# Modulations in pairs, a norm in two token parts and head reciprocals per token in a hybrid diffusion step

## What is computed

```python
def trunk_layer(x, cond, p, lam_init, ctx):
    shift1, scale1, gate1, shift2, scale2, gate2 = modulation(cond, p['w_mod'], p['b_mod'])   # 6 x 1024 per condition
    h = rmsnorm(x, p['g_mix']) * (1 + scale1) + shift1
    rq, rk, rv, rg, wq, wk, wv, dq, dk, dv, mcq, mckv, mkr = split(h @ p['w_in'])              # 2720 columns
    o_ret  = head_layernorm(bidirectional retention) * silu(rg)                               # head norm 1
    o_win  = window attention with a sink
    o_diff = rmsnorm(differential attention, p['g_diff']) * (1 - lam_init)                    # head norm 2
    o_mla  = multi-head latent attention
    merged = sum of sigmoid(h @ w_gate[n] + b_gate[n]) * (o_n @ w_branch[n])
    x = x + gate1 * (merged @ p['w_out'])
    h = rmsnorm(x, p['g_ffn']) * (1 + scale2) + shift2
    u = conv3(h @ p['w_up'] + b_up)                                                            # 2 x 2816 columns
    x = x + gate2 * ((u1 * silu(u2)) @ p['w_down'])
```

## Time and profile before

| | |
|---|---|
| median of 3 runs | 2518.57 us (2517.09 to 2520.24) |
| the profiled execution | 2514.07 us |
| its span, first to last instruction | 2512.2 us |
| mean granted TensorE clock | 0.975 |
| PE busy | 2397.0 us (95%) |
| DVE, ACT, POOL busy | 1239.9, 899.2, 754.9 us |

### The profile page before, as it was taken

The page is one execution under the profiler, slowest core; times in us unless marked ns, Lnnn a source line. Parts: engine busy times, 40 slices in busy tenths (PEclk is TensorE's granted clock), DMA queues, the critical chain, the costliest instruction groups (busy, mean ns, idle before and its releaser), DMA issues.

```text
span 2512.2 us, 38193 instructions
## 1 busy us (share of the span) xinstructions
PE 2397.0 (95%) x16007; PEld 2154.8 (86%) x16007; DVE 1239.9 (49%) x2136; ACT 899.2 (36%) x1652; POOL 754.9 (30%) x516
## 2 busy tenths in 40 slices
PE   5998999999998999999989899998999989999998
PEld 4887787778898999999968768886889989999998
DVE  4336437544235771753733461575433467536456
ACT  3424335544224431332243342555332153323221
POOL 1321131101232453544323202210113335444432
PEclk7999999999998999999989999999999989999999
DMA  8312222132321322221272132222233212222221
GB/s 284 134 37 70 95 86 89 45 101 77 105 80 52 100 68 84 68 85 59 76 243 70 36 118 63 72 74 88 68 101 94 83 51 68 84 68 85 68 68 51
DMA packets 234152, 216.45 MB, mean 86 GB/s; under 512 B 8310, under 2 KB 217598, under 8 KB 233726
## 3 DMA queue, kind: packets, MB, share of 16 engines
q1 hardware_dynamic: 225911, 193.76, 24.3%
q10 hardware_dynamic: 8071, 20.25, 2.5%
HBM read 204.92 MB, written 9.08 MB: 85 GB/s over the span
## 4 chain that ended last, share of the span: by engine, by line
PE 88%; DVE 5%; ACT 3%; issue 2%; DMA 1%; POOL 1%; ACTq 0%; DVEq 0%; SPq 0%
PE ps L744 58%; PE ps L800 12%; PE ps L839 4%; PE ps L892 2%; PE ps L871 2%; PE ps L909 2%; PE ps L755 2%; PE ps L881 2%; PE ps L1137 1%; POOL w_lo L701 1%; DVE stat L1753 1%; DVE o_rms L1959 1%; PE ps L765 1%; DMA raw<-in_w_mod 1%; PE ps L860 1%
## 5 line engine op out<-in xcount | busy, mean ns | idle before, releaser
L701 POOL TENSOR_TENSOR w_lo<-raw,w_hi 128x512 fp32r<-128x512 f32 (+1 forms) x512 | 754.7, 1504 | 1723.1 <-ACT w_hi L1283 1080.8
L744 PE MATMUL ps<-h_hi,w_hi 128*128 128x320 f32 x2432 | 631.5, 315 | 10.5 <-DVE h_lo L1700 8.0
L744 PE MATMUL ps<-h_lo,w_hi 128*128 128x320 f32 x2432 | 619.0, 310 | 0.0
L744 PE MATMUL ps<-h_hi,w_lo 128*128 128x320 f32 x2432 | 618.6, 310 | 0.0
L744 PEld LDWEIGHTS ps<-h_hi,w_hi 128*128 128x128 f32 x2432 | 425.9, 189 | 16.9 <-POOL w_lo L701 8.5
L744 PEld LDWEIGHTS ps<-h_lo,w_hi 128*128 128x128 f32 x2432 | 425.2, 189 | 0.8
L744 PEld LDWEIGHTS ps<-h_hi,w_lo 128*128 128x128 f32 x2432 | 424.7, 189 | 0.0
L1283 ACT ACTIVATE w_hi<-raw 128x2048 fp32r<-128x2048 f32 (+2 forms) x112 | 207.5, 1853 | 322.9 <-PE ps L744 241.4
L800 PE MATMUL ps<-w_hi,h_hi 128*128 128x512 f32 (+1 forms) x480 | 180.9, 377 | 17.4 <-DVE h_lo L1700 15.1
L1753 DVE TENSOR_REDUCE stat<-ps 128x1 f32<-128x640 f32 (+3 forms) x160 | 107.8, 674 | 168.7 <-PE ps L881 104.4
L1991 DVE SCALAR_TENSOR_TENSOR x<-ps,mod,x 128x128 f32<-128x128 f32 (+4 forms) x192 | 72.2, 433 | 218.8 <-PE ps L744 218.5
(11 more groups left out here) (262 smaller groups left out, 3279.3 us busy)
## 6 DMA issues: line engine op xcount, KB each, us to landing
raw<-in_w_mod SPq DMA_DIRECT2D x48, 1024.0 KB, 5.3
raw<-in_w_up SPq DMA_DIRECT2D x88, 512.0 KB, 4.8
raw<-in_w_gate SPq DMA_DIRECT2D x32, 1024.0 KB, 5.4
raw<-in_w_in SPq DMA_DIRECT2D x20, 1024.0 KB, 5.0
raw<-in_w_down SPq DMA_DIRECT2D x16, 1024.0 KB, 4.7
w_br<-in_w_branch ACTq DMA_DIRECT2D x8, 1024.0 KB, 4.9
raw<-in_w_out SPq DMA_DIRECT2D x8, 1024.0 KB, 5.1
raw<-in_w_down SPq DMA_DIRECT2D x8, 768.0 KB, 4.1
```

What stands on the lines that cost most here:

```text
L701: ins = nc.gpsimd.tensor_tensor(w_lo[s % WS][:, c0:c1], raw[u % RAW][:, c0:c1], w_hi[s % WS][:, c0:c1].bitcast(F32), ALU.subtract)
L744: ins = mm(out, w_at(w_hl[wi]), at_(x_hl[xi]), start=first and q == 0, stop=final and q == 2)
```

## The change

- The first eight modulations are made in four pairs (p, p+4), the shift and the scale of the same 256 channels. Both products go into one PSUM region (the condition columns of the second are shifted by two), one row copy, one fold with four columns, two additions and the scale of two k-steps follow. Pair 0 stands before the norm's spread and pair 1 behind it; pairs 2 and 3 and the folds of 1 to 3 stand inside `in_product(0)`. The unit order is mod 0, 4, in (0,0), mod 1, 5, 2, 6, in (0,1), mod 3, 7, and so on. The small loads move from before `in (0,1)` to before `in (1,0)`.
- At the start of layer 0 DVE copies x from PSUM, and ACT squares the unturned x with a running sum per token (five instructions of 1024 columns), so that PE's token sums aren't needed there.
- Output tiles 4 to 7 are made in two token parts, 256 and 384 tokens, all of part 0 first. The second norm is made for each part, and the first two up tiles too, part 0 of both, then part 1 of both. The first of them runs all high-high products first, then low-high, then high-low, with the sums and the spread of part 1 in between.
- Both head norms sum squares to one number per token and head (128 tokens x 20), take root and reciprocal of that, DVE copies each reciprocal 64 times along the free dimension, and PE turns the result, 128 x 128 tiles, into the layout of the outputs. In the second, the `rope` now stands before the two products.

```diff
-    units = mods(8) + win(0) + win(1) + gate(0, 0) + gate(0, 1) + win(2)
+    first, second = win(0)
+    units = mods(2) + [first] + mods(4) + [second] + mods(2) + win(1) + gate(0, 0) + gate(0, 1) + win(2)
...
+OUT_TILES = [(m, None) for m in range(4)] + [(m, 0) for m in range(4, KD)] + [(m, 1) for m in range(4, KD)]
+CUT = 2 * P
...
-                    if li == 0 and (kind, i) == ("in", (0, 1)):
+                    if li == 0 and (kind, i) == ("in", (1, 0)):
                         load_small(0)
...
+                def mod_pair(p):
+                    c0 = pair_col(p)
+                    if p >= 2:
+                        pe.wait_ge(mod_done.sem, now(mod_done, p))
+                    for second, i in enumerate((p, p + 4)):
+                        w = raw_unit("mod", i)
+                        for k in range(KD):
+                            q0 = 32 * (k % 4)
+                            last = mm(ps[q0:q0 + 32, c0:c0 + 256], cond_c[:, k, 2 - 2 * second:34 - 2 * second], w[:, k, :],
+                                      start=second == 0 and k < 4, stop=second == 1 and k >= 4)
+                        last.then_inc(mod_mm.sem, 1)
...
+                def head_sums(sq_, b):
+                    for c2 in range(2):
+                        for t in range(T):
+                            c0 = 2 * (T * c2 + t)
+                            last = mm(bank(b, c0, c0 + 2), sq_[:, c2, t * P:(t + 1) * P], c("side"), start=True, stop=True)
+                    return last
+                def turn_rstd(rec, c2, b):
+                    for t in range(T):
+                        last = tr(bank(b, t * P, t * P + P), rec[:, T * c2 + t].rearrange("p j d -> p (j d)"), ident)
+                    return last
...
-                mod_unit(0)
-                mod_unit(1)
-                pe.wait_ge(vec_done.sem, now(vec_done, 1))
-                mod_transpose(0)
+                mod_pair(0)
                 if li:
                     pe.wait_ge(x_down.sem, counts(li - 1)(x_down, 24))
-                for i in range(2, 8):
-                    mod_unit(i)
-                    mod_transpose(i - 1)
-                    if i == (2 if li else 4):
-                        token_sums(0)
-                    if i == (4 if li else 6):
-                        spread_rstd(0)
-                mod_transpose(7)
+                    token_sums()
+                fold_pair(0)
+                spread_rstd()
+                mod_pair(1)
                 pe.wait_ge(vec_done.sem, now(vec_done, 1))
-                in_product(0)
+                in_product(0, behind=[lambda: fold_pair(1), lambda: mod_pair(2), lambda: fold_pair(2), lambda: mod_pair(3), lambda: fold_pair(3)])
...
-                for c2 in range(2):
-                    ve.wait_ge(rv_act.sem, now(rv_act, c2 + 1))
-                    V.reciprocal(ret_sq[:, c2, :], ret_sq[:, c2, :]).then_inc(vstep.sem, 1)
+                def widen(rec):
+                    V.reciprocal(st5[:, 3, :], st5[:, 2, :]).then_inc(vstep.sem, 1)
+                    ve.wait_ge(vstep.sem, step())
+                    return V.tensor_copy(rec[:].rearrange("p a j d -> p (a j) d"), st5[:, 3, :].unsqueeze(2).to_broadcast([P, 4 * T, 64]))
...
-                rstd(1)
-                norm(1)
+                for m, part in OUT_TILES[:9]:
+                    take_out(m, part)
+                rstd(1, 0, 2)
+                take_out(5, 1)
+                part_norm(0, range(3))
+                take_out(6, 1)
+                part_norm(0, range(3, KD + 1))
+                take_out(7, 1)
+                rstd(2, 2, T)
+                part_norm(1, range(KD + 1))
```

More of the change, by code:

```diff
@@ L121, in shape_constants @@
     return out
+MOD_ORDER = [i for p in range(4) for i in (p, p + 4)] + list(range(8, 24))
 def weight_units():
-    mod = iter(range(24))
+    mod = iter(MOD_ORDER)
     win = lambda g: [("in", (g, half), True) for half in range(2)]
@@ L780, in spread_rstd, with part_sums, spread_part, in_product @@
                     last.then_inc(bc_mm.sem, 1)
-                def in_product(g, between=None):
+                def part_sums(part):
+                    pe.wait_ge(ss_done[1].sem, now(ss_done[1], part + 1))
+                    for t in PART_TILES[part]:
+                        last = mm(bank(4 + part, t, t + 1), ss[:, t * P:(t + 1) * P], ones[:, 0:1], start=True, stop=True)
+                    last.then_inc(ss_mm.sem, 1)
+                def spread_part(part):
+                    pe.wait_ge(diag_done.sem, now(diag_done, part + 2))
+                    for q, t in enumerate(PART_TILES[part]):
+                        last = mm(bank(6 + part, q * P, q * P + P), ones[:], diag[:, t, :], start=True, stop=True)
+                    last.then_inc(bc_mm.sem, 1)
+                def in_product(g, between=None, behind=()):
                     n, base = G_COLS[g][1], Z_BASE[g]
@@ L1094, in _ @@
                     last.then_inc(mla_mm.sem, 1)
+                pe.wait_ge(ox_done.sem, now(ox_done, 1))
+                for c2 in range(2):
+                    turn_rstd(o_rec, c2, slot()).then_inc(mla_mm.sem, 1)
                 w = raw_unit("ukv")
@@ new lines, in norm_step @@
+                def norm_step(k, done, cols, pieces):
+                    sc.wait_ge(t1_done.sem, now(t1_done, done + k + 1))
+                    if k >= 2:
+                        sc.wait_ge(h_done.sem, now(h_done, done + k - 1))
+                    i = 1 if done else 0
+                    for w, c0, c1 in pieces:
+                        ins = act_(hf[:, k % 2, c0:c1], t1[:, k % 2, c0:c1], ACT.Identity, bias=mod[:, 24 * i + k, w:w + 1],
+                                   scale=scl[:, i, k, w:w + 1])
+                    ins.then_inc(hf_done.sem, 1)
+                    sc.wait_ge(hf_done.sem, now(hf_done, done + k + 1))
+                    act_(h_hi[:, k, cols], hf[:, k % 2, cols], ACT.Copy).then_inc(hh_done.sem, 1)
@@ L1315, in norm, with part_norm @@
+                def part_norm(part):
+                    ts_ = PART_TILES[part]
+                    sc.wait_ge(ss_mm.sem, 3 * li + part + 1)
+                    act_(st5[:, 0, ts_.start:ts_.stop], bank(4 + part, ts_.start, ts_.stop), ACT.Sqrt, bias=eps_c[:], scale=1.0 / D).then_inc(rms_done.sem, 1)
+                    if part == 0:
                         round_unit()
-                        round_unit()
-                    else:
-                        round_unit()
-                    sc.wait_ge(scl_done.sem, now(scl_done, i + 1))
+                        sc.wait_ge(scl_done.sem, now(scl_done, 5))
@@ L1327, in norm @@
[L1327 to L1329 removed]
+                        norm_step(k, 8 + 8 * part, PARTS[part], ((1, CUT, TOK),) if part else ((0, 0, CTX), (1, CTX, CUT)))
                 def take_z(g, tiles=range(T)):
@@ new lines, in scale, with rstd @@
+                def scale(i, k0, n):
+                    g0 = (GMIX, GFFN)[i] + k0
+                    stt(scl[:, i, k0:k0 + n], mod[:, 24 * i + 8 + k0:24 * i + 8 + k0 + n, :], 1.0,
+                        vcol[:, g0:g0 + n].unsqueeze(2).to_broadcast([P, n, 2]), ALU.add, ALU.mult).then_inc(scl_done.sem, 1)
+                def rstd(done, t0, t1_):
+                    n = t1_ - t0
+                    ve.wait_ge(rms_done.sem, now(rms_done, done + 1))
+                    V.reciprocal(st5[:, 1, t0:t1_], st5[:, 0, t0:t1_]).then_inc(vstep.sem, 1)
```

413 lines of the change are left out of this document (237 added, 176 removed).

## The result

The changed kernel takes 2505.2 us, the median of five runs, where the kernel before takes 2518.9 beside it: a ratio of 0.9944, with a 95% interval of 0.9933 to 0.9955. A second series gave 2499.8 beside 2518.7, 0.9929 (0.9909 to 0.9949). So it is faster, by 14 to 19 us. Forecast were 41.4, and 2505.2 lies above the stated range of 2463 to 2494, and 2499.8 does too.

The account below looks back on a forecast made before the run. PE was taken to bound the kernel, except in stretches bound by chains of small steps over engines. Gains of 12.8 + 6.4 + 13.8 + 4.0 + 4.4 = 41.4 us from the median of 2518.57 gave 2477.2, range 2463 to 2494.

Parts of the forecast that it names:

- What bounds: Whole kernel: PE bounds, busy 95% of the span; around the norms and behind the retention, chains of small steps do.
- First modulations and norm: Start of each layer: in_product(0) and in_product(1) start earlier, gaining 12.8 us in layer 0 and 6.4 in layer 1.
- Retention's head norm: Behind the retention: shorter DVE work lets the rope end and PE's turns start earlier; 6.9 us a layer, 13.8 (8 to 16).
- Differential head norm: Behind the differential attention: turns of z_mq start earlier without the wait for DVE; 2.0 us a layer, 4.0 (0 to 5).
- Second norm: Output product to up tiles: norming token parts beside the tiles gains 2.2 us a layer, 4.4 (-6 to +14).
- the output product's end: Before the second norm's up tiles: the sums and spread of part 0 move this time by only 1 us.
- Small matmuls: Split output and up tiles: matmuls of 256 columns take 0.12 us, so splitting costs PE nothing.
- (a): Rival: weight line becomes the bound, halving the first norms' gain and leaving the second norm at nothing; 2491 us, chance 0.16.
- (b): Rival: everything counted as late is in time, in the first norms and behind the output products; 2461 us, chance 0.12.
- (c): Rival: PE's turns behind the retention don't wait for the head norm, so the 13.8 is lost; 2491 us, chance 0.03.
- (d): Rival: clock stays low throughout in_product(0) and the first up tiles, adding 101.4 us; 2579 us, chance 0.05.

Follow-up runs that it names:

- whole_mended: Changed kernel with its second norm in whole tiles again, ACT's weight rounding behind that norm's root kept as in the kernel before; 2487.8 us, 0.9878 of before.
- heads: Kernel before with only the change's two head norms (reciprocals per token and head); 2492.7 us, 0.9901 of before.
- ret_head: Kernel before with only the retention's head norm changed; 2500.6 us, 0.9929 of before.
- after_again: The changed kernel run once more, no line changed, for a second trace; median 2499.8 us.
- take_later: Changed kernel with DVE taking each modulation pair behind norm step 2p instead of 2p-1, so behind the low part of h; 2483.2 us, 0.9863 of before.
- whole_later: Changed kernel with both edits: second norm in whole tiles, and DVE taking each pair behind the low part of h; 2470.9 us, 0.9811 of before.
- short_both: take_later with POOL making only the first quarter of the low parts of units out 3 and up 2 (output wrong); 2464.6 us, 0.9783 of before.
- short_up2: take_later with POOL making only the first quarter of unit up 2's low part (output wrong); 2472.5 us, 0.9814 of before.
- late_split: take_later with only out tiles 6 and 7 split into token parts, tiles 0 to 5 whole; 2483.7 us, 0.986 of before.
- short_out3: take_later with POOL making only the first quarter of unit out 3's low part (output wrong); 2470.0 us, 0.981 of before.

## Why the prediction was wrong, point by point

- **What bounds, and that the change takes no work from PE.** Right. So was the look for chains of small steps, and the time at which the first products can start: 34.3 for 32.3 in layer 0, and in layer 1 1261.4, which is 1270.6 on the scale of before, for 1270.5.
- **First modulations and norm, 12.8 + 6.4.** The gain measured 5.0 and 1.0 in the traces, and 4.9 in all by the medians (whole_mended against heads). The step that failed is "PE needs 3.4 for a k-step, so the norm keeps ahead, except where a step waits for its pair's scale". I asked when the scale reaches ACT, and not what else stands behind `take_pair` on DVE. With the take one step later the forecast's own number for `in_product(1)` is met in layer 0 (72.75 for 73.3), layer 1 does 4 us better (1293.32, 1307.4 on the scale of before, for 1311.5), and the part is worth 21.8 us (2492.7 less 2470.9), above the 19.2 forecast.
- **Retention's head norm, 13.8.** The mechanism was right and the size low: 18.5 by the medians, 16.1 to 19.3 by the chains of after, ret_head and heads. Two terms were too small. The turns start 5.8 us earlier against the first gate chunk, not 5.0; and my sum ended with the copies of `wk_t`, where the chunk right behind the turns, at 206.96, still took 3.89 us before, for 3.52 now. With the faster turns (3.43 to 1.75 us, as forecast) layer 0 is 8.1 ahead one chunk later, for 6.9. The rest comes and goes: 70 us later a gate chunk took 4.82 in before and 3.72 in after, but 5.46 in after_again and 5.34 in take_later, both with the new head norm. So it is not shown that the clock falls less often there.
- **Differential head norm, 4.0.** Measured 7.9 by the medians, 0.8 and 5.0 from before to after, 4.0 and 4.9 from ret_head to heads. The term was read in layer 0 alone, whose turns of `z_mq` took 2.39 us. In layer 1 of before, the same turns behind the same wait, from PE's timeline, and both places in the stretch table:

```profile
1750.21 4.05 PE L1112 MATMUL ps<-const,z_mq 128*96 128x128 f32 x20 [2.09 <-DVE z_mq L1716]
```
```profile
1750.00:1755.00 5.00, 4.05 (x20) 3.65 (x20) 0.16 (x1) 2.79 (x4) 0.00 (x0) 0.66 0.58 181
...
515.00:520.00 5.00, 3.35 (x27) 3.10 (x28) 1.00 (x5) 3.48 (x5) 0.00 (x0) 1.00 0.67 201
```

  The granted clock was 0.66 in one and 1.00 in the other. The stage from `in_product(3)` to the output product with the old norm took 428.4 and 432.5 us in before, 431.6 and 432.5 in ret_head: I had read the quickest of the four. In heads it takes 427.6 in both layers. The step that was mis-sized is the clock behind that wait, which my sum put at nothing.
- **Second norm, 4.4.** It made the kernel 12.0 to 17.4 us slower; with the forecast gain the miss is 16 to 22, the largest. The step that failed is the output product's end, "a time that the sums and spread of part 0 move by 1": it moved by 4.7 (702.93 to 764.2 for 56.61). In terms: unit out 3's low part was not in the count (2.4 us of wait a layer); nor was its clock (4.4 more, 1.5 of it behind up tile 2, where the forecast had the wait of 2.69 right as 2.6 and nothing behind it); and the norm's steps on 256 tokens come every 1.22 us, not every 1.05. The first two make 6.8 of the 8.1 us a layer between forecast (-2.2) and trace (+5.9). The steps (chain, after):

```profile
767.09 0.88 ACT hf L1418 x2
...
768.31 0.87 ACT hf L1418 x2
```

  Small matmuls were priced right: those of 256 columns start 0.119 apart, for 0.12.
- **Rivals.** (a), the weight line, is nearest to what came: I gave it "the second norm at nothing" and half of the first norms. In the second norm it did not just take the gain but made a loss, and in the first DVE's order was the bound; the weight line shows there only once that order is mended (4.3 us of waits in take_later). (b), all in time, stood at 2461; take_later with both low parts short comes to 2464.6, though with larger head norms and smaller gains elsewhere. (c) is refuted. (d), the low clock, came as a multiplier of the waits and not as a state: the mean over 33 to 81 us is 0.89 in the changed kernel.
- **The sum.** By medians the parts are 4.9 + 26.4 - 17.4 = 13.9, where 19.2 + 17.8 + 4.4 were forecast. That they add up to the measured 13.7 proves nothing, as each part is the difference of two neighbours between before and after. By the medians all four terms lay outside their own ranges, two above and two below, so by luck 8.6 us of what two parts missed are made up by the other two. And the ranges, added in quadrature as stated, give -14.5 and +11.3, not -16 and +13.

The Trainium skill, TensorE: Matmul & The Clock Gate, section "HAM oscillation — how this bites in real kernels", describes a wait that throws PE back to the low clock for what follows. The trace agrees on single waits: 6.48 us for the k-step behind 3.44 us of idling. I had used it for a rival only, and it belonged in the price of every wait of that kind.

Left open: why one execution drops the clock behind a wait of 2 us and another does not, and the 1.2 us at the end of the kernel. From the last cut on, before, heads, ret_head, whole_mended, whole_later and short_both take 39.9 to 40.1 us, short_up2 40.4, and after, after_again, take_later, late_split and short_out3 41.0 to 41.1. So it goes with the parts and their waits, in a way that no run explains.

## What to carry to other kernels

When an instruction that waits is put into an engine's program, list what stands behind it there and who waits for that; a wait that comes back to the same engine over two others costs each time round. When tiles are cut smaller or reordered, redo the count for every weight unit's line (slot free, load, round, low part) against the work that now covers it, not only for the units near the stage that is meant to gain. And do not price a short wait of PE at its length alone: the two measured here, of 2.4 and 2.7 us, were worth 2.9 and 1.6 times that. Read it in every layer in which it occurs, because the clock behind it is part of it.

## What the runs showed of the hardware

The same wait doesn't always cost the same: behind the wait of 2.7 us before up tile 2 the granted clock was 0.66 in take_later and late_split and 1.00 in short_out3, in both layers of each. What before the wait decides it, no run shows. The clock can also fall without a wait right ahead: twenty small sums took 2.13 us, and in layer 1 of after the twelve matmuls right behind them took 4.36 us where layer 0's took 2.88, although PE had no idle time there. In ret_head it is the other way round, 4.17 in layer 0 and 2.88 in layer 1, so the sums alone are not shown to be the cause. The row in layer 1 of after:

```profile
1398.48 2.13 PE ps L871 x20
1400.61 4.36 PE ps L853 x12
```

The widening copy of 1280 columns, for which I had bounds of 0.8 and 3.3 us, took 0.83 in all four places. POOL was idle then, so its contention wasn't seen.
